# Nine weight slots instead of seven for the experts' weight stream, with row buffers folded into a free tile

## The reference, cut to what matters

```python
def _moe(h, w_router, w_gate, w_up, w_down):        # h: 256 x 1024, 8 experts, hidden width 3584
    logits = h @ w_router
    top_logits, top_idx = lax.top_k(logits, 2)       # each token goes to two experts
    gates = jax.nn.softmax(top_logits, axis=-1)
    # tokens sorted by expert
    hid = silu(xs @ w_gate[e]) * (xs @ w_up[e])      # 1024 x 3584 each
    ys = hid @ w_down[e]                             # 3584 x 1024
    # ys times its gate, added to its token's row

x = x + _moe(_rmsnorm(x, ffn_norm), ...)
return _rmsnorm(x, final_norm)
```

## Time and profile before

| | us |
|---|---|
| median of 3 runs | 1805.62 |
| lowest and highest run | 1803.22, 1808.26 |
| the profiled execution's own time | 1803.67 |
| its span, first to last instruction | 1801.8 |

### The profile page before, as it was taken

One profiled execution on the slowest core, in us unless ns is written; L12 is line 12 of the kernel. 1 busy time (PEld: TensorE's weight loads), 2 busy tenths in 40 slices (PEclk: granted clock), 3 DMA queues, 4 the chain that ended last, 5 costly groups with the idle time before them and its releaser, 6 DMA issues.

```text
span 1801.8 us, 25011 instructions
## 1 busy us (share of the span) xinstructions
PE 1704.4 (95%) x10932; PEld 835.7 (46%) x10932; DVE 441.2 (24%) x823; ACT 281.5 (16%) x558; POOL 202.2 (11%) x175
## 2 busy tenths in 40 slices
PE   8999999999999999999899977999998889999976
PEld 4576654456644454556444322444443334444322
DVE  3633333213662410236331000110100001011011
ACT  1210221223410100343201010110101001011011
POOL 0210000004467700034000000000000000000000
PEclk9999999999999999999899999999999999999998
DMA  9742217744225353433569999999999999999995
GB/s 329 251 136 95 82 44 227 247 156 155 94 94 187 140 210 111 143 140 122 218 238 405 409 404 410 408 404 410 403 409 408 406 410 403 409 394 405 410 404 229
DMA packets 169914, 493.47 MB, mean 274 GB/s; under 512 B 15599, under 2 KB 24192, under 8 KB 169545
## 3 DMA queue, kind: packets, MB, share of 16 engines
q1 hardware_dynamic: 161003, 469.67, 68.3%
q0 software_dynamic: 3632, 12.98, 2.0%
q10 hardware_dynamic: 5166, 9.16, 1.4%
HBM read 483.64 MB, written 13.13 MB: 276 GB/s over the span
## 4 chain that ended last, share of the span: by engine, by line
PE 78%; DMA 16%; DVE 3%; issue 1%; ACT 1%; POOL 1%; SPq 0%; ACTq 0%; DVEq 0%; POOLq 0%
PE bank L1271 24%; PE bank L2995 17%; DMA ring<-in_moe_w_up 9%; PE bank L3054 7%; PE bank L3011 7%; PE bank L1283 7%; DMA ring<-in_moe_w_down 4%; PE bank L3064 4%; PE bank L537 2%; PE bank L612 2%; PE bank L1294 1%; DMA shift_rows<-ring 1%; DMA ring<-shift_rows 1%; PE bank L1860 1%; PE bank L3027 1%
## 5 line engine op out<-in xcount | busy, mean ns | idle before, releaser
L1271 PE MATMUL bank<-ring,work 128*128 128x512 f32 (+3 forms) x1248 | 519.1, 573 | 6.0 <-DVE work L2217 2.8
L2995 PE MATMUL bank<-ring,work 128*64 128x512 f32 x1792 | 402.6, 607 | 33.9 <-DMA ring<-in_moe_w_up 33.3
L1271 PEld LDWEIGHTS bank<-ring,work 128*128 128x128 f32 x1248 | 232.2, 191 | 264.9 <-issue 243.0
L2995 PEld LDWEIGHTS bank<-ring,work 128*64 128x64 f32 x1792 | 131.5, 140 | 288.3 <-issue 287.5
L3054 PE MATMUL bank<-ring,work 128*64 128x512 f32 x896 | 201.2, 599 | 12.7 <-DMA ring<-in_moe_w_down 12.7
L3054 PEld LDWEIGHTS bank<-ring,work 128*64 128x64 f32 x896 | 63.9, 138 | 137.3 <-issue 137.3
L3011 PE MATMUL bank<-ring,work 128*32 128x256 f32 x2240 | 125.0, 380 | 0.0
L1283 PE MATMUL bank<-ring,work 128*128 128x512 f32 (+1 forms) x264 | 108.8, 567 | 0.7 <-POOL work L2594 0.7
L3179 DVE TENSOR_TENSOR work<-work,bank 64x512 f32<-64x512 f32 x56 | 38.7, 692 | 288.6 <-ACT work L3095 256.0
L3011 PEld LDWEIGHTS bank<-ring,work 128*32 128x32 f32 x2240 | 70.8, 110 | 60.8 <-issue 16.2
L3151 POOL DMA_DIRECT2D expert_rows<-work x7 | 3.6, 519 | 740.6 <-DVE work L3288 553.8
(11 more groups left out here) (431 smaller groups left out, 1389.3 us busy)
## 6 DMA issues: line engine op xcount, KB each, us to landing
ring<-in_moe_w_gate SPq DMA_DIRECT2D x56, 2048.0 KB, 19.3
ring<-in_moe_w_up SPq DMA_DIRECT2D x56, 2048.0 KB, 16.4
ring<-in_moe_w_down SPq DMA_DIRECT2D x56, 2048.0 KB, 19.1
ring<-in_w_in SPq DMA_DIRECT2D x20, 2048.0 KB, 8.4
ring<-in_w_out SPq DMA_DIRECT2D x6, 2048.0 KB, 7.8
ring<-in_dense_w_gate SPq DMA_DIRECT2D x5, 2048.0 KB, 9.5
ring<-in_dense_w_up SPq DMA_DIRECT2D x5, 2048.0 KB, 7.8
ring<-in_dense_w_down SPq DMA_DIRECT2D x5, 2048.0 KB, 7.9
```

Of the source, the lines that this page charges most:

```text
L1271: mm = pe.matmul(banks(j)[:, 0:width], x[:, k0 + kt, tt * P:(tt + 1) * P], w[:, kt, c0:c0 + width], start=first and n == 0, stop=last and ...
L2995: mm = pe.matmul(out[rows, :], xgT[:, half * tiles + k, 0:64], w[n][:, k, cols], start=(half == 0 and k == 0), stop=last)
```

## The change

Two more slots, numbers 7 and 8, lie at the top of `main`. The plan loads nine instead of seven loads ahead: loads 0 to 4 keep their slots and issue points, loads 5 and 6 go to slots 7 and 8 and are issued directly behind load 4, and loads 7 and 8 take the slots of the output projection that loads 5 and 6 had. In `experts_first` load n waits for load n - 9, and the slot of a load is its number modulo nine in the list `first_slots`.

To make room, `final_gain` no longer has a place of its own: it is loaded into the top of slot 8 when the last load held there (159) has been given back, as the last issue of SP's loop, behind load 167. `taken` and the four `fetched` buffers become one buffer, which together with `ys` lies in `uT`. So a fetch now waits until the last expert's rows have been turned (`gathered`) and, from the second on, until DVE has added the one before (`fetched_added`). DVE's fourth add stands after its branch for the next expert's rows, which is empty in the last expert, so its place among DVE's operations is the same.

```diff
+FIRST_SLOTS = 9
+        self.more_at = room - (FIRST_SLOTS - SLOTS) * SLOT
+    def slot_at(self, slot):
+        if slot < SLOTS:
+            return self.ring[:, slot, :]
+        at = self.more_at + (slot - SLOTS) * SLOT
+        return self.main.whole[:, at:at + SLOT]

+def first_slot(core, e, i):
+    return core.first_slots[(LOADS * e + i) % FIRST_SLOTS]

 def experts_first(...):
-    taken = take(DM)
-    fetched = [[take(DM) for _ in range(NT)] for _ in range(2)]
+    rows_of = Region(core.uT.rearrange("p k t -> p (k t)"), NT * DM)
+    taken, ys = rows_of.take(DM), rows_of.take(DM)
+    fetched = taken
...
-    ys = take(DM)
...
+    kept_load = LOADS * NE - FIRST_SLOTS
...
     def _(sp):
-        for n in range(SLOTS, NE * LOADS):
+        for n in range(FIRST_SLOTS, NE * LOADS):
...
-            sp.wait_ge(core.weights_used, used0 + n - SLOTS + 1)
-            sp.dma_start(pair_slot(core, i), pair_weight(a, expert if e else 0, i))\
-              .then_inc(core.landed[slot_of(core, i)], 16)
+            sp.wait_ge(core.weights_used, used0 + n - FIRST_SLOTS + 1)
+            sp.dma_start(pair_slot(core, e, i), pair_weight(a, expert if e else 0, i))\
+              .then_inc(core.landed[first_slot(core, e, i)], 16)
+        sp.wait_ge(core.weights_used, used0 + kept_load + 1)
+        sp.dma_start(final_gain, spread(a["final_norm_2"], P)).then_inc(final_in, 16)
...
     def _(pool):
+        pool.wait_ge(gathered, 2 * NE)
         for n in range(2):
             for tt in range(NT):
                 if n + tt:
                     pool.wait_ge(rows_fetched, 16 * (2 * n + tt))
-                pool.indirect_dma_start(fetched[n][tt], None, rows_dram,
+                    pool.wait_ge(fetched_added, 2 * n + tt)
+                pool.indirect_dma_start(fetched, None, rows_dram,
...
     def add_fetched(n, tt):
-            step(dve.scalar_tensor_tensor(out=rows, in0=fetched[n][tt], ...
+            dve.scalar_tensor_tensor(out=rows, in0=fetched, ...).then_inc(fetched_added, 1)
+            dve.wait_ge(fetched_added, 2 * n + tt + 1)
...
-                    if p == PAIRS:
-                        add_fetched(1, 1)
             if e + 1 < NE:
                 take_gathered(e + 1)
+            else:
+                add_fetched(1, 1)

 program:
-        for i in range(SLOTS):
-            core.add_weights(pair_weight(a, 0, i), 4, DM, slot=core.moe_slots[i])
+        core.first_slots = core.moe_slots[0:5] + [7, 8] + core.moe_slots[5:7]
+        for i, s in enumerate(core.first_slots):
+            n = core.add_weights(pair_weight(a, 0, i), 4, DM, slot=s)
...
-        final_gain = main.take(DM)
+        final_gain = main.whole[:, whole_main - DM:whole_main]
-        core.slots_now = SLOTS
+        core.slots_now = FIRST_SLOTS
             core.load_weights(sp, everything, most=core.moe_used + 3)
             sp.wait_ge(*m.scratch_left)
-            sp.dma_start(final_gain, spread(a["final_norm_2"], P)).then_inc(final_in, 16)
             core.load_weights(sp, everything)
```

More of the change, by code:

```diff
@@ L190, in __init__ @@
         self.main = Region(ctx.enter_context(nc.sbuf_tensor("work", [P, room], F32)), room)
+        self.more_at = room - (FIRST_SLOTS - SLOTS) * SLOT
         self.ps = [ctx.enter_context(nc.psum_tensor(f"bank{i}", [P, BANK], F32)) for i in range(BANKS)]
-        self.landed = [ctx.enter_context(nc.semaphore(f"weights_landed{i}")) for i in range(SLOTS)]
+        self.landed = [ctx.enter_context(nc.semaphore(f"weights_landed{i}")) for i in range(FIRST_SLOTS)]
         self.weights_used = ctx.enter_context(nc.semaphore("weights_used"))
@@ L196, in __init__ @@
         self.consumed = 0
-        self.uses = [0] * SLOTS
-        self.last_in_slot = [-SLOTS + i for i in range(SLOTS)]
+        self.uses = [0] * FIRST_SLOTS
+        self.last_in_slot = [-FIRST_SLOTS + i for i in range(FIRST_SLOTS)]
         self.slots_now = SLOTS
@@ L2868, in pair_weight, with pair_slot, experts_first @@
     return expert_weight(a, e, i)
-def pair_slot(core, i):
-    return core.ring[:, slot_of(core, i), :].rearrange("p (k n) -> p k n", n=BANK if 4 * PAIRS <= i < 2 * NC else DM)
-def experts_first(core, a, r, xn, gain):
+def first_slot(core, e, i):
+    return core.first_slots[(LOADS * e + i) % FIRST_SLOTS]
+def pair_slot(core, e, i):
+    return core.slot_at(first_slot(core, e, i)).rearrange("p (k n) -> p k n", n=BANK if 4 * PAIRS <= i < 2 * NC else DM)
+def experts_first(core, a, r, xn, gain, final_gain, final_in):
     nc, ps, h, ident = core.nc, core.ps, core.h, core.ident
@@ L2909, in experts_first @@
         "ys_by_scalar", "rows_written", "rows_fetched", "where_ready", "dest_ready", "rows_spread", "taken_in",
-        "scattered", "added", "flag_ready", "order_ready", "ranked_ready", "vector_steps"))
+        "scattered", "added", "flag_ready", "order_ready", "ranked_ready", "vector_steps", "fetched_added"))
     narrow_before = [NC * sum(NARROW[:e]) for e in range(NE + 1)]
@@ L2928, in landed @@
         def landed(e, i):
-            s = slot_of(core, i)
-            pe.wait_ge(core.landed[s], landed0[s] + 16 * (3 * e + i // SLOTS))
+            s = first_slot(core, e, i)
+            pe.wait_ge(core.landed[s], landed0[s] + 16 * ((LOADS * e + i) // FIRST_SLOTS))
         pending = [0]
@@ L2973, in pair @@
                 landed(e, i + 1)
-                w = [pair_slot(core, i), pair_slot(core, i + 1)]
+                w = [pair_slot(core, e, i), pair_slot(core, e, i + 1)]
                 for form in (pair_wide, pair_narrow)[::-1 if half else 1]:
@@ L3043, in down @@
             landed(e, 2 * NC + c)
-            w = pair_slot(core, 2 * NC + c)
+            w = pair_slot(core, e, 2 * NC + c)
             for form in (down_wide, down_narrow)[::1 if c % 2 == 0 else -1]:
@@ L3194, in add_fetched @@
             rows = h[:, tt, :]
-            step(dve.scalar_tensor_tensor(out=rows, in0=fetched[n][tt], scalar=r.weight[:, tt, n:n + 1], in1=rows,
-                                          op0=ALU.mult, op1=ALU.add))
+            dve.scalar_tensor_tensor(out=rows, in0=fetched, scalar=r.weight[:, tt, n:n + 1], in1=rows,
+                                     op0=ALU.mult, op1=ALU.add).then_inc(fetched_added, 1)
+            dve.wait_ge(fetched_added, 2 * n + tt + 1)
         def add(tt, banks):
@@ L3294, in experts_first @@
     r.flag_ready, r.first_added = (flag_ready, 1), added
-    core.moe_landed = [n + 48 * NE for n in core.moe_landed]
+    for i, s in enumerate(core.first_slots):
+        core.moe_landed[s] += 16 * len(range(i, LOADS * NE, FIRST_SLOTS))
 def experts_rest(core, a, r, xn, gain):
@@ L3332, in _ @@
         with when(sp, r.flag):
+            sp.wait_ge(core.weights_used, used0)
             for n in rounds:
@@ L3549, in program @@
         core.moe_slots[3:3] = [5, 6]
-        for i in range(SLOTS):
-            core.add_weights(pair_weight(a, 0, i), 4, DM, slot=core.moe_slots[i])
-        core.moe_landed = [0] * SLOTS
-        for i in range(SLOTS):
-            core.moe_landed[core.moe_slots[i]] = core.plan[core.moe_used + i]["landed"]
+        core.first_slots = core.moe_slots[0:5] + [7, 8] + core.moe_slots[5:7]
+        core.moe_landed = [0] * FIRST_SLOTS
+        for i, s in enumerate(core.first_slots):
+            n = core.add_weights(pair_weight(a, 0, i), 4, DM, slot=s)
+            core.moe_landed[s] = core.plan[n]["landed"]
         core.slots_now = 3
@@ L3652, in program @@
         main.back(low_at)
-        final_gain = main.take(DM)
-        kept = main.at
+        final_gain = main.whole[:, whole_main - DM:whole_main]
         final_in = ctx.enter_context(nc.semaphore("final_in"))
-        core.slots_now = SLOTS
+        core.slots_now = FIRST_SLOTS
         @core.block.sync
@@ L3671, in program @@
         route(core, r, logits)
-        experts_first(core, a, r, xn, gains["ffn_norm_2", 1])
+        main.size = core.more_at
+        experts_first(core, a, r, xn, gains["ffn_norm_2", 1], final_gain, final_in)
+        main.size = whole_main - DM
         experts_rest(core, a, r, xn, gains["ffn_norm_2", 1])
```

4 lines of the change are left out of this document (2 added, 2 removed).

## The result

The changed kernel takes 1794.64 us in the median (1792.45 to 1799.41), against 1804.03 (1803.22 to 1808.26) for the kernel before when more runs of it are counted in. The ratio is 0.9945, with an interval of 0.9932 to 0.9957: 9.9 us faster, between 7.8 and 12.3. The profiled execution, the fastest of the five, took 1792.45 us with a span of 1790.5. The forecast was 1794.1 for the median and 1790.3 for the span.

A forecast was written before the change was run, and what follows sets the result against it. The last landing of the weight stream was taken to set the end. Two loads' 10.3 us plus 1.2 for the thin place made 11.5: span 1801.8 to 1790.3, median forecast 1794.1 us, range 1790.5 to 1799.2.

The forecast's parts named there:

- Two loads leave the stream: Expert stage: two loads land in the gap before it, leaving 159 loads behind the first permit instead of 161; gain 10.3 us.
- The reasoning on permits: SP's loop: the first issue, now load 9, stays at 917.88; no transfer meets a later permit than before.
- The end of the stream: Last expert: last wait for weights ends at 1778.72, taken as the last landing, with 8.72 us of matrix work behind it.
- The lead lasts: From PE's first wait for weights on, PE gets each load 10.3 us sooner, and releases come as much earlier.
- The thin place in the seventh expert: Full expert from 1574 to 1689: 401 GB/s should rise to 407; gain 1.2 us, between 0 and 1.7.
- Costs put at nothing: final_gain behind load 167, one buffer for fetched rows, and taken and ys in uT: each taken as 0 us.
- The fetches' cover: Last expert: chained fetches done by 1770.5, 17.0 us before the copy of the last result at 1787.53; cost 0.
- The start that slips: Rival: mixer's last products run slower beside the two early loads, nothing is gained; 1803 to 1806 us, chance 0.08.
- The chained fetches: Rival: fetches in the last expert end last, taking 17 us more than their bounds; 1800 to 1808 us, chance 0.03.
- Loads into slots 7 and 8: Rival: some 36 loads into the other tile run slower than those into the ring; over 1810 us, chance 0.04.
- The tail: Rival: PE's last 32 products all stay at the lower clock, 5.3 us more; 1796 to 1799 us, chance 0.10.
- the signs listed: Profile after: four issues at 856 to 862, no idle 875 to 880, expert 2 at 1112.9, last wait ending about 1767.

The follow-up runs named there:

- e2_eight: The changed kernel with eight slots instead of nine: median 1800.45 us, ratio 0.9978 to the kernel before, stage length 876.12 us.
- e1_seven: The changed kernel with seven slots instead of nine, all other edits kept: median 1804.64 us, ratio 0.9997 to the kernel before.
- e6_short_later: The kernel before with loads 40 and 41, in expert 1, cut to a sixteenth: median 1795.94 us, ratio 0.9958 to the kernel before.
- e4_short: The kernel before, seven slots, with loads 7 and 8 cut to a sixteenth: median 1800.67 us, ratio 0.9981 to the kernel before.
- e3_nine_late: The changed kernel with loads 7 and 8 issued only when load 0 is given back: median 1805.31 us, ratio 1.0007 to the kernel before.
- e8_start_late: The changed kernel with 32 unused products ahead of the first gather: median 1801.67 us, ratio 0.9983 to the kernel before, stage length 870.14 us.
- e7_fetch_five: The changed kernel with the fourth fetch made five times in a row: median 1804.74 us, ratio 0.9997 to the kernel before.

## Why the prediction was right, step by step

*Two loads leave the stream: right.* 10.3 us were worked out, and the stage length fell by 10.32. One load gives 4.65 (e2_eight), none gives 0 (e1_seven), both cut inside the stream give 9.48 (e6_short_later). The reasoning on permits was a needed part of it, as e4_short shows: without a permit for the next load the same two loads gave 3.2.

*The end of the stream: read 5 us too early, at no cost to the sum.* The prediction took the last wait, 1778.72, for the last landing. In the kernel before load 166 lands at 1778.6 and load 167 at 1783.6, while PE works on 166. So 161 loads took 5.38 us each and not 5.35, and behind the last landing stand 3.65 us of products and not 8.72. Both ends moved alike, so the gain is the same.

*The lead lasts: right.* It was 10.1 us at expert 2 and 10.3 at the last wait.

*The thin place in the seventh expert, 1.2 us: wrong.* That stretch was to rise from 401 to 407 GB/s. It rose to 404, and not because of the lead: e3_nine_late with no lead shows 404 as well, and its stage length is 881.11, no shorter than with seven slots (880.51 and 880.77). With seven slots the rate is 401 (before) and 402 (e1_seven). So more slots do fill 2 or 3 of the 6 GB/s, which is 0.8 us of transfer at most, and none of it reached the end. The term should have been 0. In the changed kernel one stretch of that expert stays thin, 361 GB/s in the 10 us from 1605.7; what lowers the rate there was not tried.

*The sum came out right by an offset.* The span fell by 11.3 us and the forecast said 11.5, but the parts were 10.3 in the stage and 1.1 ahead of it. The latter has no cause in the change: load 4 goes out at 855.37 after and at 856.91 before, and over all the profiles shown here at 855.20 to 858.07, with the changed kernel itself at 857.97 in its second profile. The ratio, which averages over more executions, says 9.9 us, nearer to 10.3 than to 11.5. That the median came within 0.6 us of the forecast is luck in the same way: the forecast was taken from a median of 1805.62 before, which more runs put at 1804.03, and the changed kernel's second set of runs has 1796.66.

*Costs put at nothing: right.* One buffer, the tiles in uT and final_gain behind the stream cost nothing together (e1_seven). final_gain took 21.6 us to land, at 1773.5, and the last norm's first use of it is at 1784.71, so its cover was 11 us. The fetches' cover was put at 17.0 us; the fourth add ended at 1753.89, 22.2 us ahead of the copy. Of the 5.2 us more, 3.0 are the fetch, whose row could be added 7.8 us after its issue where 10.8 were allowed, and 2.2 are its issue, which came earlier than the shifted times said. The Trainium skill says in DMA: Bandwidth & Descriptors, Queues, rings and completion order, that an engine takes turns between the queues with work. The trace agrees: in the last expert weight loads landed 20.1 to 26.4 us after their issue, and the fetches in 7.5 to 8.3.

*The rivals.* The start that slips was priced right, one for one by the length (e8_start_late), and did not occur. The chained fetches decide from 22 us of delay, not 17 (e7_fetch_five). Loads into slots 7 and 8 are not slower: their medians from issue to landing are 23.8 to 24.1 us, those of the loads into the ring 23.6 to 24.3, and a gain of two whole loads leaves no room for it. The tail gave nothing back: 8.75 us of last products against 8.72.

*Of the signs listed,* the four issues, the filled gap, the fetches with adds between and the end of the last wait (1767.29, about 1767 said) came. Expert 2 started at 1112.03 where 1112.9 was said, and the last expert at 1677.43 where it was 1678, both on a start that was 1.1 us early. 407 GB/s did not come.

## What to carry to other kernels

Where one stream of transfers sets the end, as here, one more slot was worth one load's time, once, and only because two things held: the load landed in time that was idle before the stream starts, and the first load of the stream kept the permit that the one in its place had. A deeper look-ahead alone was worth nothing, in a stream that already ran at its full rate. To price such a change, measure from the stage's first instruction to its last one: it repeated within 0.3 us where the span moved by 4. And look for the last landing, not for the last wait: a load can land while the matrix engine is busy with the one before, and then no wait shows it.

## What the runs showed of the hardware

- A transfer of 96 or 64 rows of 4 KB into as many partitions was no cheaper than one of 128 rows: 7.85 MB took the same 1.4% of the engines as 9.16 MB, the rate of all transfers fell to 354 GB/s in the 5 us beside one of them, and the stage grew by 2.2 us.
- The last two loads of 2 MB in a queue, issued 5.0 us apart, landed 5.0 us apart (1767.2 and 1772.2), one load's time at the full rate. Pieces of 0.5 MB of the last load landed 1.3 us apart, and the last of them within 0.1 us of when the whole load landed, counted from the first product.
- Fetches on POOL's queue landed in 7.5 to 8.3 us beside weight loads that took 20.1 to 26.4, and the last one of e7_fetch_five, with the weights all there, in 4.4.
- Over 115 us of a full expert the transfers ran at 401 to 407 GB/s in the kernels measured for it, and at 404 to 413 in most stretches of 10 us with no rows going in or out beside the weights. By the 358 GB/s of the Trainium skill (SBUF — State Buffer, A bandwidth-pool intuition that's wrong) the two loads would have been 11.7 us, an estimate; the stage length fell by 10.3.
